# Two layers of mixed branches and an expert block: the recurrence prepared beside retention, the branch sum in place, expert gates in pairs

## The reference, cut to what matters

```python
h = rms_norm(x, ln_mix_pre[l]); z = h @ w_in[l]
z_q, z_kv, z_g, z_ret, z_rwkv, z_conv, z_gate = split_cols(z, IN_SIZES)
# attention, retention, rwkv7 recurrence, short convolution, each 256 wide
merged = sum_m sigmoid(z_gate)[m] * (branches[m] @ w_branch[l, m])      # four branches
x = x + rms_norm(merged @ w_mix_out[l], ln_mix_post[l])
# cross attention to mem, then the MLP of the layer
```

## Time and profile before

| | us |
|---|---|
| median of 3 runs (lowest to highest) | 2187.3 (2186.85 to 2193.8) |
| the profiled execution, its own time | 2196.44 |
| its span in the profile | 2194.5 |
| TensorE busy | 1961.5 (89%) |
| VectorE busy | 1445.3 (66%) |
| ScalarE busy | 1148.3 (52%) |
| mean granted clock of TensorE | 0.934 of full speed |

### The profile page before, as it was taken

How to read it: one execution, slowest core, us unless ns; L and a number is a source line. 1 busy time by engine, 2 the same in 40 slices (tenths; PEclk the granted TensorE clock), 3 DMA queues, 4 the chain that set the end, 5 groups by cost and what they waited for, 6 DMA issues and landing times.

```text
span 2194.5 us, 30396 instructions
## 1 busy us (share of the span) xinstructions
PE 1961.5 (89%) x13010; PEld 1789.1 (82%) x13010; DVE 1445.3 (66%) x1431; ACT 1148.3 (52%) x1240; POOL 70.0 (3%) x94
## 2 busy tenths in 40 slices
PE   4988996988999888998897999897679999999997
PEld 3978996988998877997897999796568888888885
DVE  3677646635555667746644555656659989998995
ACT  3533333544444543233544444464358888888883
POOL 0000003000000000003000000000000000000000
PEclk9998998998999889999899999898779999999998
DMA  6333355533554333346342555332249999999993
GB/s 259 124 126 113 110 182 205 198 115 135 192 192 155 149 118 128 112 158 241 140 181 96 190 196 183 144 116 95 78 191 352 379 347 358 372 362 369 359 365 148
DMA packets 64525, 440.88 MB, mean 201 GB/s; under 512 B 7372, under 2 KB 7372, under 8 KB 14592
## 3 DMA queue, kind: packets, MB, share of 16 engines
q1 hardware_dynamic: 55296, 399.63, 48.6%
q0 software_dynamic: 8096, 35.30, 4.2%
q10 hardware_dynamic: 992, 3.93, 0.5%
...
...
## 4 chain that ended last, share of the span: by engine, by line
PE 68%; DVE 18%; ACT 9%; DMA 2%; issue 1%; POOL 1%; ACTq 0%; DVEq 0%; POOLq 0%
PE psum L188 66%; ACT hl L198 4%; DVE ring_low L202 3%; DVE arena L212 2%; DVE ht L202 2%; DVE hl L202 2%; ACT arena L198 2%; DVE rounded L212 2%; DVE rounded L202 2%; PE psum L192 2%; DVE arena L202 2%; POOL arena L202 1%; ACT gn L198 1%; ACT rounded L198 1%; DVE arena L225 1%
## 5 line engine op out<-in xcount | busy, mean ns | idle before, releaser
L202 DVE TENSOR_TENSOR hl<-ring,hl 128x2048 fp32r<-128x2048 f32 (+1 forms) x190 | 430.2, 2266 | 349.9 <-ACT hl L198 349.6
L188 PE MATMUL psum<-ht,hl 128*128 128x256 f32 x4992 | 630.5, 288 | 15.6 <-DVE hl L202 9.9
L188 PEld LDWEIGHTS psum<-ht,hl 128*128 128x128 f32 x4992 | 616.3, 195 | 26.5 <-DVE hl L202 10.5
L198 ACT ACTIVATE hl<-ring 128x2048 fp32r<-128x2048 f32 (+1 forms) x286 | 535.9, 1895 | 170.0 <-PE psum L188 143.6
L198 ACT ACTIVATE arena<-psum 128x512 f32<-128x512 f32 (+7 forms) x242 | 123.4, 510 | 470.2 <-PE psum L188 446.8
L188 PE MATMUL psum<-hl,ax 128*128 128x512 f32 (+1 forms) x1608 | 356.2, 358 | 5.9 <-DVE ax L202 4.8
L188 PEld LDWEIGHTS psum<-hl,ax 128*128 128x128 f32 x1608 | 268.0, 194 | 47.6 <-DVE ax L202 5.5
L188 PE MATMUL psum<-arena 128*128 128x128 f32 (+6 forms) x1520 | 201.3, 303 | 34.3 <-ACT arena L198 23.6
L202 DVE TENSOR_TENSOR ring_low<-ring,hl 128x2048 fp32r<-128x2048 f32 x96 | 215.4, 2286 | 21.4 <-ACT hl L198 21.3
L188 PEld LDWEIGHTS psum<-arena 128*128 128x128 f32 (+2 forms) x1520 | 184.4, 188 | 46.8 <-ACT arena L198 25.3
L188 PE MATMUL psum<-hl,ht 128*128 128x256 f32 (+1 forms) x1056 | 133.7, 289 | 29.3 <-DVE ht L212 26.5
...
## 6 DMA issues: line engine op xcount, KB each, us to landing
...
```

The lines of the kernel that those rows point to most:

```text
L188: return Nothing() if self.e is None else self.e.matmul(o, a, b, start=start, stop=stop, skip_group_check=skip_group_check)
L198: return self.e.activation(o, a, f, bias=bias, scale=scale)
L202: return Nothing() if self.e is None else self.e.tensor_tensor(o, a, b, op)
```

## The change

- **Memory.** `cl` moves to the start of the arena, beside `lw` and `aa`, and `mid` and retention's tiles are laid out anew, so that the tiles of the scans and the scaled tiles no longer overlap what retention still needs.
- **Order.** On VectorE the scans and midpoints stand ahead of "rkr", the scaled tiles and padded copies between "rsq" and the root of retention's variance. On ScalarE the exponentials stand ahead of the retention outputs. The copies of "tm" wait for `oT` 1 in addition. TensorE makes three fills ahead of the lora products (before: two), none ahead of "kknorm", one (before: two) ahead of "tm", and a new one between M and U 0. The fills of ScalarE and VectorE are placed to match.
- **Roots.** The three inverse roots of a layer (kk's norm, retention's variance, y's variance) are exp(-0.5 ln(v + eps)) on ScalarE; their reciprocals on VectorE go. For kk's norm eps is a new constant, `tiny`, 1e-36, and min with 1e12 takes the place of max with 1e-12.
- **Branch sum.** The gate reads of the first three branches are issued behind "y" 1, the last behind the last gate store. Merge and sum are made in place in `Gt`. VectorE makes the first branch's merges ahead of y's norm, two of the second's behind it, and interleaves merge, sum and low part at the end.
- **Experts.** The gates times two are split once into a high and a low fp32r column (`gp`). `place` makes them for its own expert, two products of two columns each, and ScalarE adds the two columns up with an accumulating copy (`gs`). The scratch tiles `l3` and `oh1` move to the place of the constants `lev`.

The diff, without context and empty lines, and with up to twelve leading blanks taken off; left out are the constant `tiny`, the tile `mo.gp` (2 x 32 x 2, in `rounded`) and the flag `after` of VectorE's `ts`:

```diff
@@ -397,11 +397,11 @@
-L.lw, L.aa, L.hb = al(2, 256), al(2, 256), al(4)
+L.lw, L.aa, L.hb, L.cl = al(2, 256), al(2, 256), al(4), al(4, 128)
+assert ar["n"] <= 7 * 257
...
-L.cl, L.mid = al(4, 128), al(4, 8)
...
@@ -418,16 +418,17 @@
-L.midv = L.mid.rearrange("p (j c) n -> p j c n", c=2)
...
-L.raw, L.gs, L.gth, L.rv = al(4, 256), al(2, 256), al(2, 256), al(2, 256)
-L.cs, L.dec = al(2, 256), al(4, 384)
-L.rq, L.rk, L.tmp4, L.att = al(4, 256), al(2, 256), al(2, 256), al(4, 384)
+L.tmp4, L.gth, L.cs = al(2, 256), al(2, 256), al(2, 256)
+L.dec, L.att, L.rk, L.rv = al(4, 384), al(4, 384), al(2, 256), al(2, 256)
+L.raw, L.rq, L.gs = al(4, 256), al(4, 256), al(2, 256)
+L.mid = al(4, 8)
...
+L.midv = L.mid.rearrange("p (j c) n -> p j c n", c=2)
...
@@ -479,8 +480,10 @@
-        mo.lg, mo.oh, mo.l3, mo.s4, mo.gw = al(2, 36), al(2, 4), al(2, 32), al(2, 16), al(2, 32)
-        mo.oh1, mo.mk, mo.posm, mo.flg = al(2, 32), al(2, 32), al(2, 32), al(4)
+        mo.lg, mo.oh, mo.s4, mo.gw = al(2, 36), al(2, 4), al(2, 16), al(2, 32)
+        mo.mk, mo.posm, mo.flg = al(2, 32), al(2, 32), al(4)
+        lev = SHAPE_COLS.at["lev"][0]
+        mo.l3, mo.oh1 = (cst[:, lev + 64 * i:lev + 64 * i + 64].rearrange("p (t n) -> p t n", t=2) for i in range(2))
...
@@ -755,8 +759,7 @@
-    fill()
-    fill()
+    fill(3)
...
@@ -799,7 +801,7 @@
-    fill(2)
+    fill()
...
@@ -1159,11 +1162,9 @@
-        if i == 0:
-            for n in range(4):
-                ins = mm(psum[:, b, 256 + n:257 + n],
-                         [(mo.OH[g % 2][:, t, 128 * n:128 * n + 128].bitcast(F32), mo.gw[:, t, e + n:e + n + 1])
-                          for t in range(2)])
+        pe.wait_ge(s_dve, V["gp"])
+        ins = mm(psum[:, b, 256:258], [(mo.OH[g % 2][:, t, 128 * i:128 * i + 128], mo.gp[:, t, e, :])
+                                       for t in range(2)])
...
@@ -1342,8 +1343,15 @@
-    act(o, half(banks[name]), ACT.Sqrt, *name, bias=C(eps) if eps else 0.0, scale=scale)
+    act(o, half(banks[name]), ACT.Sqrt, *name, bias=C(eps), scale=scale)
...
+def inverse_root(o, eps, scale, *name):
+    ac.wait_ge(s_pe, P[name])
+    act(o, half(banks[name]), ACT.Ln, *name, "log", bias=C(eps), scale=scale, after=False)
+    gone(*name)
+    act(o, o, ACT.Exp, *name, scale=-0.5)
...
@@ -1470,7 +1478,7 @@
-    fill()
+    fill(2)
...
@@ -1480,9 +1488,14 @@
-    fill()
-    root(L.t2, None, 1.0, "kknorm", l)
-    fill()
+    inverse_root(L.t2, "tiny", 1.0, "kknorm", l)
+    ac.wait_ge(s_dve, V["cl", l])
+    act(L.Ep, L.cl, ACT.Exp, "Ep", l, after=False)
+    act(L.Em, L.cl, ACT.Exp, "Em", l, scale=-1.0, after=False)
+    fill()
+    ac.wait_ge(s_dve, V["clq", l])
+    act(L.Eq, L.cl, ACT.Exp, "Eq", l, after=False)
+    act(L.mid[:, :, 3:6], L.mid[:, :, 0:3], ACT.Exp, "mid", l, after=False)
...
@@ -1490,24 +1503,18 @@
-    root(L.rrb, "eps5", 1.0 / 64, "rvar", l)
-    fill()
+    inverse_root(L.rrb, "eps5", 1.0 / 64, "rvar", l)
+    fill(2)
...
-    ac.wait_ge(s_dve, V["cl", l])
-    act(L.Ep, L.cl, ACT.Exp, "Ep", l)
-    act(L.Em, L.cl, ACT.Exp, "Em", l, scale=-1.0)
-    ac.wait_ge(s_dve, V["clq", l])
-    act(L.Eq, L.cl, ACT.Exp, "Eq", l)
-    act(L.mid[:, :, 3:6], L.mid[:, :, 0:3], ACT.Exp, "mid", l)
-    fill(2)
+    ac.wait_ge(s_dve, V["oT", 1, l])
...
-    fill()
+    fill(2)
...
@@ -1537,19 +1544,21 @@
+    unit()
...
-    root(L.yrb, "eps64", 1.0 / 64, "yvar", l)
+    inverse_root(L.yrb, "eps64", 1.0 / 64, "yvar", l)
...
-    for m in range(4):
+    for m in range(3):
...
-        act(hTv[0][:, js, :], L.mg[:, js, :], ACT.Copy, "merged", jj, l, scale=0.5)
+        act(hTv[0][:, js, :], L.Gt[:, 8 * BRANCHES[0] + 2 * jj:8 * BRANCHES[0] + 2 * jj + 2, :], ACT.Copy, "merged", jj, l,
+            scale=0.5)
...
@@ -1812,8 +1821,7 @@
-        if e % 4 == 0:
-            act(mo.gs[:, e:e + 4], psum[:, beside + 1, 256:260], ACT.Copy, "gs", e // 4, scale=2.0, after=False)
+        act(mo.flg[:, 2:4], psum[:, beside + 1, 256:258], ACT.Copy, "gs", e, acc=mo.gs[:, e:e + 1], after=False)
...
@@ -1830,7 +1838,7 @@
-        ac.wait_ge(s_act, A["gs", e // 4])
+        ac.wait_ge(s_act, A["gs", e])
...
@@ -2126,11 +2136,16 @@
-    ve.wait_ge(s_act, A["g2", l])
+    ve.wait_ge(s_act, A["a2", l])
...
-    ts(L.aa, L.aa, 0.5, 0.5, MUL, ADD)
-    fill()
-    ve.wait_ge(s_act, A["kknorm", l])
+    ts(L.aa, L.aa, 0.5, 0.5, MUL, ADD, after=False)
+    for i in range(4):
+        scan(L.cl[:, i, :], C("ones"), L.lwc[:, i, :])
+    ts(L.mid[:, :, 0:1], L.cl[:, :, 63:64], 1.0, None, MUL, None)
+    tt(L.mid[:, :, 1:2], L.cl[:, :, 127:128], L.mid[:, :, 0:1], SUB)
+    copy(L.mid[:, :, 2:3], L.cl[:, :, 127:128])
+    tt(L.cl, L.cl, wide(L.mid[:, :, 0:1], 128), SUB, "cl", l)
+    ve.wait_ge(s_pe, P["kknorm", l])
...
@@ -2138,57 +2153,49 @@
-    ts(L.t2, L.t2, 1e-12, None, MAX, None)
-    rec(L.t2, L.t2)
-    tt(L.kk, L.kk, L.t2, MUL)
-    fill()
+    fill()
+    ve.wait_ge(s_act, A["kknorm", l])
+    stt(L.kk, L.t2, 1e12, L.kk, ALU.min, MUL)
+    ve.wait_ge(s_act, A["Em", l])
+    tt(L.cl, L.cl, L.lwc, SUB, "clq", l)
...
-        tt(L.att[:, h, :], psum[:, banks["att", h, l], 0:384], L.dec[:, h, :], MUL, "att", h, l)
+        tt(L.att[:, h, :], psum[:, banks["att", h, l], 0:384], L.dec[:, h, :], MUL, "att", h, l, after=False)
...
+    fill()
...
-    tt(L.bon, half(banks["bonus", l]), L.v, MUL)
+    tt(L.bon, half(banks["bonus", l]), L.v, MUL, after=False)
...
-    fill()
...
+    f4 = "p j (c n) -> p (j c) n"
+    ve.wait_ge(s_act, A["mid", l])
+    tt(L.rP.rearrange(f4, c=2), L.r.rearrange(f4, c=2), L.Ep, MUL)
+    tt(L.t1, L.kk, L.aa, MUL)
+    tt(L.bP.rearrange(f4, c=2), L.t1.rearrange(f4, c=2), L.Em, MUL)
+    tt(L.kP.rearrange(f4, c=2), L.k2.rearrange(f4, c=2), L.Em, MUL)
+    stt(L.aP.rearrange(f4, c=2), L.kk.rearrange(f4, c=2), -1.0, L.Eq, MUL, MUL)
+    ve.wait_ge(s_pool, G["aPz0", l])
+    ve.wait_ge(s_dve, V.n)
+    for h in range(4):
+        es = slice(64 * (h % 2), 64 * (h % 2) + 64)
+        copy(L.aPz[es, h, :], L.aP[es, h // 2, :])
+        copy(L.rPz[es, h, :], L.rP[es, h // 2, :], "aPz", l)
+    fill()
...
-    rec(L.rrb, L.rrb)
...
+    fill()
...
-    fill()
-    for i in range(4):
-        scan(L.cl[:, i, :], C("ones"), L.lwc[:, i, :])
-    ts(L.mid[:, :, 0:1], L.cl[:, :, 63:64], 1.0, None, MUL, None)
-    tt(L.mid[:, :, 1:2], L.cl[:, :, 127:128], L.mid[:, :, 0:1], SUB)
-    copy(L.mid[:, :, 2:3], L.cl[:, :, 127:128])
-    tt(L.cl, L.cl, wide(L.mid[:, :, 0:1], 128), SUB, "cl", l)
-    ve.wait_ge(s_act, A["Em", l])
-    tt(L.cl, L.cl, L.lwc, SUB, "clq", l)
-    fill()
-    f4 = "p j (c n) -> p (j c) n"
-    tt(L.rP.rearrange(f4, c=2), L.r.rearrange(f4, c=2), L.Ep, MUL)
-    tt(L.t1, L.kk, L.aa, MUL)
-    tt(L.bP.rearrange(f4, c=2), L.t1.rearrange(f4, c=2), L.Em, MUL)
-    tt(L.kP.rearrange(f4, c=2), L.k2.rearrange(f4, c=2), L.Em, MUL)
-    ve.wait_ge(s_act, A["mid", l])
-    stt(L.aP.rearrange(f4, c=2), L.kk.rearrange(f4, c=2), -1.0, L.Eq, MUL, MUL)
-    ve.wait_ge(s_pool, G["aPz0", l])
-    for h in range(4):
-        es = slice(64 * (h % 2), 64 * (h % 2) + 64)
-        copy(L.aPz[es, h, :], L.aP[es, h // 2, :])
-        copy(L.rPz[es, h, :], L.rP[es, h // 2, :], "aPz", l)
-    fill()
...
@@ -2252,39 +2260,55 @@
+    first = L.Gt[:, 8 * BRANCHES[0]:8 * BRANCHES[0] + 8, :]
+    def merge(m, jj):
+        gsl = L.Gt[:, 8 * m + 2 * jj:8 * m + 2 * jj + 2, :]
+        ve.wait_ge(s_gin[m], 16 * (l + 1))
+        ve.wait_ge(s_pe, P["merge", m, jj, l])
+        stt(gsl, gsl, 1.0, half(banks["merge", m, jj, l]), ADD, MUL, "merge", m, jj, l, after=False)
+        gone("merge", m, jj, l)
+    unit()
+    for jj in range(4):
+        merge(BRANCHES[0], jj)
...
-    rec(L.yrb, L.yrb)
...
+    for jj in range(2):
+        merge(BRANCHES[1], jj)
...
+    for jj in range(2, 4):
+        merge(BRANCHES[1], jj)
...
-    for n, m in enumerate(BRANCHES):
-        unit()
-        ve.wait_ge(s_gin[m], 16 * (l + 1))
-        for jj in range(4):
-            gsl = L.Gt[:, 8 * m + 2 * jj:8 * m + 2 * jj + 2, :]
-            js = slice(2 * jj, 2 * jj + 2)
-            dst = L.mt if m else L.mg
-            ve.wait_ge(s_pe, P["merge", m, jj, l])
-            if n >= 2:
-                ve.wait_ge(s_pool, G["sum", BRANCHES[n - 1], jj, l])
-            stt(dst[:, js, :], gsl, 1.0, half(banks["merge", m, jj, l]), ADD, MUL, "merge", m, jj, l)
-            gone("merge", m, jj, l)
+    unit()
+    for jj in range(4):
+        merge(BRANCHES[2], jj)
+    unit()
+    unit()
+    def low(jj):
+        js = slice(2 * jj, 2 * jj + 2)
+        ve.wait_ge(s_act, A["merged", jj, l])
+        stt(hTv[1][:, js, :], first[:, js, :], 0.5, hTv[0][:, js, :].bitcast(F32), MUL, SUB, "merged", l, after=False)
...
+        merge(BRANCHES[3], jj)
...
-        tt(L.mg[:, js, :], L.mg[:, js, :], L.mt[:, js, :], ADD, "sum", jj, l)
-    for jj in range(4):
-        js = slice(2 * jj, 2 * jj + 2)
-        ve.wait_ge(s_act, A["merged", jj, l])
```

(42 more changed lines are left out.)

15 lines of the change are left out of this document (5 added, 10 removed).

## The result

| | before | after |
|---|---|---|
| median (lowest to highest), the first comparison | 2190.55 (2186.85 to 2197.89), 4 runs | 2119.04 (2115.13 to 2120.46), 4 runs |
| the profiled execution, its own time | 2196.44 | 2118.27 |
| its span | 2194.5 | 2116.5 |
| mean granted clock of TensorE | 0.934 | 0.957 |

The ratio of the times is 0.9667, with a 95% interval of 0.9635 to 0.9698: 3.3% faster. The forecast was 2124, its range 2108 to 2150. A later comparison of the same program gave 2122.17 (2115.71 to 2123.88, 5 runs) beside 2193.17 for before, ratio 0.9663 [0.9645, 0.9682].

What follows compares the result with a forecast made beforehand. It held that time goes where TensorE waits or works at half clock. Gains of 2 x 16.6 + 2 x 7.8 + 14.3 = 63 us from a median of 2187.3 gave 2124 us, range 2108 to 2150.

Steps and rivals of the forecast that it cites:

- Part 1: From attention to the doubling steps: reordering removes TensorE's long stops and their half clock, 16.6 us a layer, bounds 8 to 22.8.
- no stop over 3 us: Sign for the stretch from attention to the doubling steps: near 75 us, clock near 1.00, no TensorE stop above 3 us.
- Part 2: Branch sum: mix begins 9.1 us sooner, less 1.3 us given back; 7.8 us a layer, bounds 2 to 11.
- Back go 1.3 us: Behind the branch sum: ScalarE reloads the root's table for the memory norm, ahead of TensorE's transposes, costing 1.3 us.
- VectorE's queue sets this: Branch sum: VectorE's queue, not TensorE, sets the mix's start at 358.9, with splits now ahead of the last merges.
- rival C: Branch sum: POOL's adds, eight at 3.2 us, bound it; 1.7 us a layer gained, 2136 us; chance 0.08.
- only sums and splits have two in the buffer: Branch sum: argument against POOL's adds binding, since a merge has one input in PSUM and so does not block POOL.
- Part 3: Expert loop: heavy steps shorten to 17.2 us, added matmuls cost 0.3 a plain step; 14.3 us gained, bounds 2 to 21.
- all expert steps between 16.4 and 17.3 us, no half clock in them: Sign for the expert loop: every step's time in this range, with TensorE never at half clock.
- B: Front of the recurrence: scans ahead of retention make it late, half clock returns; 8 us a layer, 2141 us; chance 0.16.
- D: Expert loop: DMA keeps its pace, so shorter heavy steps gain 0; 2138 us; chance 0.11.
- E: Expert loop: small matmuls drop TensorE to half clock in every step; slower than before, 2200 us; chance 0.03.

Runs made afterwards that it cites:

- bonus_behind: The changed kernel with TensorE's projection bc 0 ahead of the bonus sum instead of behind it: 2117.62 us, ratio 0.9652 to before.
- late_split: The changed kernel with VectorE's split for the mix's second unit moved behind the last low part of the branch sum: 2124.38 us, ratio 0.9682 to before.
- adds_vector: The changed kernel with POOL's eight adds a layer made by VectorE: 2121.56 us, ratio 0.9669 to before.
- gates_x4: The changed kernel with the two small gate products of an expert made four times: 2139.19 us, ratio 0.9748 to before.
- changed_again: The changed kernel once more, unaltered, for a second trace: 2122.17 us.
- bonus_late: The changed kernel with both the projection ahead of the bonus sum and the mix's second split behind the last low part: 2118.53 us, ratio 0.9658 to before.
- experts_only: The kernel before with only the expert change, gates as two fp32r columns made for each expert: 2180.77 us, ratio 0.9949 to before.

## Why the prediction held, step by step

The medians fell by 71.5 us (2190.55 to 2119.04), 8.5 more than the 63 of the sum. The prediction started from 2187.3, 3 us under this median of before, and that brought 2124 closer.

**Part 1: right, in mechanism and terms.** TensorE's work was 69.41 us; 68.4 and 1.6 of half clock, 70.0, were forecast. The stops were 4.2 us against 4.6: "lor" 0.59 for 0.5, "rkr" 3.15 for 2.6, "rmean" 0.47 for 0.5, and the 1.0 for handovers did not come. The half clock behind the "rkr" stop was 1.7 us for 1.6: the bonus sum and its 48 products take 8.38 us, and 6.69 in the trace of before, where no stop stands ahead of them. `bonus_behind` shows that the stop causes it. The sign "no stop over 3 us" was missed by 0.15. The copies ended at 161.5 with the stretch beginning at the same time, forecast 160; TensorE asked at 169.5, forecast 168. What the prediction had not separated: it counted 7.1 us of reciprocals as what keeps VectorE from binding. With them the stretch is only 1.0 us longer; VectorE's order alone carries it.

**Part 2: the sum right within 0.4 us, two of its terms wrong.** In the time of the old trace the mix began at 359.3, forecast 358.9. (1) "Back go 1.3 us" for the table load ahead of the memory norm: it went unseen. ScalarE in the changed kernel:

```profile
352.38 1.28 ACT L198 ACT_TABLE_LOAD   x1
353.70 0.29 ACT L198 ACTIVATE arena<-arena 128x1 f32<-128x1 f32 x1
```

VectorE makes a split until 353.4 before it hands over the variance, so the load lies under it; the transposes follow the mix's first 96 products after 0.29 us, as before. The Trainium skill, "ScalarE: Activation LUTs", section "What ACT_TABLE_LOAD costs", gives 2.66 us a switch with its drain, and by it the prediction estimated the root of y 1.4 us late. In the trace each of these loads is followed by its activation 1.29 or 1.30 us after its start with nothing between, and no drain shows. (2) "VectorE's queue sets this": the chain from the products' end to the mix passes through POOL's adds for nearly all of 318.8 to 334.2:

```profile
321.03 3.25 POOL arena L202
...
324.41 1.32 POOL arena L202
...
325.86 3.17 POOL arena L202
...
329.17 3.14 POOL arena L202
```

Its eight adds took 18.0 us, forecast 17.0, with three meetings of 3.2 as forecast. VectorE waited 1.1 us for them. `late_split` shows that POOL sets the start of the mix: with 3.3 us taken off VectorE, it moved by what one add of POOL became shorter. `adds_vector` shows that this costs next to nothing: without POOL, VectorE has the mix start 0.5 us later. So rival C, which had 0.08, was true in its mechanism and nearly without price.

That the sum came out within 0.4 us is in part luck, for its terms erred both ways. The merges beside the branches took 2.47 to 2.66 us for four and not 3.06, and VectorE was 1.1 us ahead of the forecast when the second branch's merges were done (337.1 for 338.2 in the old time). The split beside POOL then took 1.5 us more than its 2.29. From the last split to the mix it took 10.5 us, forecast 9.5, with the two waits and a low part of 1.75 us in it: "only sums and splits have two in the buffer" left out the low parts.

The section "Who interferes with whom" ("SBUF — State Buffer" in the Trainium skill) says that the order of issue decides which of the two engines waits for the other. The rows show both directions: POOL's add rises from 1.3 to 3.2 us, and the split beside it from 2.29 to 3.78.

**Part 3: right, terms a little off.** Added per plain step 0.2 us, forecast 0.3 (0.11 a record by `gates_x4`). Heavy steps 17.11, forecast 17.2; the six of before took 18.14 to 21.38, on average 20.0. The last went to 15.79 as said. 15.35 against 14.3. One sign failed: "all expert steps between 16.4 and 17.3 us, no half clock in them". The first step of the loop took 20.35 us at a clock of 0.83, for 18.70 at 0.91 before, and 20.3 to 20.4 in the traces of `changed_again`, `bonus_late` and `experts_only`. That is a loss of 1.7 us inside the 15.35; its cause was not tested.

**What the sum left out.** It took the untouched stretches as constant. They are not: 10.4 us fell there in the profiled pair, and the next trace of the same program was 5.5 us longer, nearly all of it there. The forecast of 2124 lies over the first median and just over the second; its range held both. Rivals B, D and E are excluded for this kernel: no stop ahead of "tm"; heavy steps that did get shorter, with the DMA at 400 GB/s in the step of 15.79; no half clock in the plain steps behind the first.
